# Unread matmuls at the head of TensorE's program, and another order of the first three weight slabs

## The reference, cut to what matters

```python
def hybrid_layer(x, ..., norm_g, w_in, ...):
    h = rms_norm(x, norm_g)          # x * rsqrt(mean(x*x) + 1e-6) * g
    z = h @ w_in                     # 1024 x 14848 columns, cut into eleven parts
    (c_glu, c_gate, r_q, r_k, r_v, ...) = split(z)
    y_conv = conv_module(c_glu, ...) # a * sigmoid(b), 31 taps, layer norm, silu
    y_ret = retention_branch(r_q, r_k, r_v, ...)
    ...
```

## Time and profile before

| | |
|---|---|
| Median of three runs | 2975.7 us |
| Profiled execution, its own time | 2974.69 us |
| Its span, first to last instruction | 2972.9 us |
| Around the span | 1.8 us |
| TensorE busy | 2943.8 us (99%) |
| VectorE busy | 1893.7 us (64%) |
| GpSimd busy | 1439.3 us (48%) |
| ScalarE busy | 1284.4 us (43%) |
| HBM traffic | 91 GB/s over the span |

### The profile page before, as it was taken

The page is one execution under the profiler, slowest core; times in us unless marked ns, Lnnn a source line. Parts: engine busy times, 40 slices in busy tenths (PEclk is TensorE's granted clock), DMA queues, the critical chain, the costliest instruction groups (busy, mean ns, idle before and its releaser), DMA issues.

```text
span 2972.9 us, 43739 instructions
## 1 busy us (share of the span) xinstructions
PE 2943.8 (99%) x15008; PEld 2456.0 (83%) x15008; DVE 1893.7 (64%) x2852; ACT 1284.4 (43%) x2068; POOL 1439.3 (48%) x1056
## 2 busy tenths in 40 slices
PE   8999999999999999999999999999999999999998
PEld 6888888878888888888887888888888888798997
DVE  7985577874524598577697634367772343784756
ACT  4233333484332423333347633246563323553634
POOL 5443443455555444443355555543444445555745
PEclk9999999999999999999999999999999999999999
DMA  4322322213333332222221233332223323333322
GB/s 153 99 72 77 92 78 83 88 44 100 92 99 102 120 99 80 90 84 71 81 90 58 78 97 102 92 121 71 78 71 99 106 79 120 99 100 100 108 92 86
DMA packets 73870, 271.34 MB, mean 91 GB/s; under 512 B 8192, under 2 KB 9088, under 8 KB 73088
## 3 DMA queue, kind: packets, MB, share of 16 engines
q1 hardware_dynamic: 70560, 254.84, 27.9%
q10 hardware_dynamic: 3168, 14.61, 1.4%
HBM read 264.17 MB, written 5.24 MB: 91 GB/s over the span
## 4 chain that ended last, share of the span: by engine, by line
PE 85%; issue 7%; POOL 5%; DVE 1%; ACT 1%; DVEq 0%; POOLq 0%; ACTq 0%
PE gem L574 15%; PE gem L576 15%; PE gem L575 15%; POOL wlo L471 5%; PE xp L1149 2%; PE xp L1150 2%; PE xp L1151 2%; PE gem L1009 2%; PE gem L1011 2%; PE gem L1010 2%; PE gem L701 2%; PE gem L699 2%; PE gem L700 2%; PE gem L819 2%; PE gem L821 1%
## 5 line engine op out<-in xcount | busy, mean ns | idle before, releaser
L471 POOL TENSOR_TENSOR wlo<-raw,whi 128x512 fp32r<-128x512 f32 x820 | 1135.4, 1407 | 1357.0 <-ACT whi L1234 1357.0
L1234 ACT ACTIVATE whi<-raw 128x1024 fp32r<-128x1024 f32 x410 | 432.6, 1057 | 493.9 <-PE gem L576 332.6
L574 PE MATMUL gem<-zhi,whi 128*128 128x512 f32 x1312 | 512.1, 390 | 0.3 <-DVE zlo L2006 0.3
L576 PE MATMUL gem<-zhi,wlo 128*128 128x512 f32 x1312 | 510.7, 389 | 0.0
L575 PE MATMUL gem<-zlo,whi 128*128 128x512 f32 x1312 | 510.5, 389 | 0.0
L574 PE MATMUL gem<-hhi,whi 128*128 128x512 f32 x1104 | 430.2, 390 | 0.0
L576 PE MATMUL gem<-hhi,wlo 128*128 128x512 f32 x1104 | 429.6, 389 | 0.0
L575 PE MATMUL gem<-hlo,whi 128*128 128x512 f32 x1104 | 429.5, 389 | 0.0
L574 PEld LDWEIGHTS gem<-zhi,whi 128*128 128x128 f32 x1312 | 246.3, 188 | 51.8 <-DVE zlo L2006 0.8
L576 PEld LDWEIGHTS gem<-zhi,wlo 128*128 128x128 f32 x1312 | 246.3, 188 | 51.6
L575 PEld LDWEIGHTS gem<-zlo,whi 128*128 128x128 f32 x1312 | 246.3, 188 | 50.8
(11 more groups left out here) (511 smaller groups left out, 6016.2 us busy)
## 6 DMA issues: line engine op xcount, KB each, us to landing
raw<-in_slabs SPq DMA_DIRECT2D x446, 512.0 KB, 3.6
U<-in_slabs SPq DMA_DIRECT2D x32, 512.0 KB, 3.7
U<-in_x SPq DMA_DIRECT2D x4, 512.0 KB, 6.6
U<-in_x ACTq DMA_DIRECT2D x1, 2048.0 KB, 10.1
xsave<-U ACTq DMA_DIRECT2D x1, 2048.0 KB, 6.7
U<-xsave ACTq DMA_DIRECT2D x1, 2048.0 KB, 10.0
out_y<-yr SPq DMA_DIRECT2D x8, 256.0 KB, 2.2
tab<-in_tab_ret ACTq DMA_DIRECT2D x2, 512.0 KB, 4.8
```

What stands on the lines that cost most here:

```text
L471: part = pool.tensor_tensor(wlo[:, k % 4, c], raw[:, k % 2, c], whi[:, k % 4, c].bitcast(f32), O.subtract)
L574: pe.matmul(o, wh, hi, start=(n == 0), stop=False)
L576: mm = pe.matmul(o, wl, hi, start=False, stop=(n == len(terms) - 1))
L1234: act.activation(whi[:, k % 4, :], raw[:, k % 2, :], A.Copy).then_inc(hi_done, 1)
```

## The change

TensorE executes 24 matmuls of the 128x128 constant of ones with itself (float32, 128 columns) into the first 128 columns of bank 3 of `xp`, as soon as that constant is set and ahead of its wait for the rounded copy; nobody reads the result. And the order of the first slabs becomes: rows 0 to 7 of slab 0, each as it arrives; rows 0 to 4 of slab 1; the square sum; rows 5 to 7 of slab 1; slab 2; slab 3. No other engine's list is changed.

```diff
+WARM = 24
...
             pe.sem_inc(slab_done, 1)
             pe.wait_ge(consts, 1)
+            for n in range(WARM):
+                pe.matmul(xp[:, 3, 0:P], ones[:, :], ones[:, :], start=True, stop=True)
             pe.wait_ge(ones_ready, 1)
...
                 else:
-                    plain_rows(0, 0, 5, arriving=True)
+                    plain_rows(0, 0, NT, arriving=True)
                     plain_rows(1, 0, 5)
                     square_sum(L, 0)
-                    plain_rows(0, 5, NT, arriving=True)
                     plain_rows(1, 5, NT)
                     plain_rows(2, 0, NT)
                 plain_rows(3, 0, NT)
```

## The result

The changed kernel took 2980.1 us in the median of 22 runs (2979.1 to 2980.8), the kernel before 2974.6 us in 22 runs (2974.3 to 2976.2). The ratio is 1.0017 with a 95% interval of 1.0011 to 1.0023: slower by 0.17% (the medians differ by 5.5 us), less than the 0.2% named in the prediction, and inside the stated range of 2976.9 to 2981.6. The forecast was +4.0 us. The span of the profiled execution grew from 2972.9 to 2978.2, by 5.3 us.

What follows compares the result with a forecast made beforehand. TensorE, busy 99%, was taken as the bound, with VectorE a second limit at bank 2. Matmuls 0, clock 0, TensorE's idle time +2.0, VectorE's lateness +2.0: 2975.7 + 4.0 = 2979.7 us, range 2976.9 to 2981.6.

Steps and rivals of the forecast that it cites:

- The 24 matmuls cost nothing, and end near 9: At TensorE's start, 48 records fit the 8.8 us wait for tile 0, ending between 6.5 and 12.8: cost 0.
- a rise in the middle: Within the 24 matmuls, the clock rises after some 4 us: 17 records take 4 us, the other 31 take 3.6.
- The estimate of 7.8 us at the upper level: For the 24 matmuls at the head: four float32 passes of about 81 ns each, against 5.6 us by the row.
- The clock gives nothing: Rows 0 to 2 of slab 0 shorten to 0.68 from 1.3 us, but TensorE then waits for tiles: gain 0.
- 0 for the clock: The clock's term in the forecast sum, for rows 0 to 2 at the start: no gain on the path.
- The rival of the clock that stays down: At the start, matmuls fail to raise the clock, still lower at 12.8: +6.2, 2981.9 us or more; chance 0.10.
- The order costs TensorE 2.0 us itself: Waiting for slab 0's rows 5 to 7 before slab 1 starts the fifth slab at 38.85 instead of 36.87.
- VectorE's lateness comes through at bank 2: At the value products, VectorE, 4.0 us late from the square sum, releases bank 2 late: +2.0 more for TensorE.
- one of about 2 us: Announced sign: a new wait of TensorE for VectorE at the value products, about 2 us, near 130.5.
- The matmuls do nothing at all: Rival: the clock falls back before tile 0, rows 0 to 2 unchanged, loss still 4.0; shares the forecast's 0.62.

Runs made afterwards that it cites:

- the filled kernel: The changed kernel plus 2, 2, 2, 6, 6 and 2 further unread matmuls behind rows 0 to 5 of slab 0; median 2978.6 us, ratio 1.0013.
- the one with only the chain late: Against the old order with 24 matmuls and gaps filled: square sum moved behind rows 5 to 7 of slabs 0 and 1; median 2978.6 us, ratio 1.0013.

## Why the prediction was right, and where it was off

**The number.** The total was nearer than the reasoning deserved. The forecast of 2979.7 us lies 0.4 under the measured 2980.1, but it stood on a median of 2975.7, 1.1 us above that of the 22 later runs; the change itself was forecast at +4.0 and measured at +5.5. That the two misses nearly cancel is luck.

**The 24 matmuls cost nothing, and end near 9.** Right: 8.81, for 8.8 us of idle start. The measured time for the whole train, 7.8 us, is within the bounds of 5.6 and 11.3, and the estimate of a rise in the middle was close.
The estimate of 7.8 us at the upper level that the prediction drew from the Trainium skill (page "TensorE: Matmul & The Clock Gate", section "Back-to-back issue gap") meets the same number by chance: the first 7 records took 1.66 us (0.98 to 2.64), 0.237 each, which is the lower level, and the other 41 took 0.15 each in the mean.

**The clock gives nothing.** Right as to the gain: with and without the matmuls the new order takes 2980.1 and 2980.3 us. But the sum says "0 for the clock", and lets a loss come only from a clock that is still down at 12.8. That is **the step that failed**: it priced the clock's rise and not its fall behind row 3. All rows after 13.35 were taken at the upper level, because in the trace of the kernel before they were; but there slab 1 filled the waiting time of tiles 5 to 7, and the change empties that stretch, while the short rows 0 to 2 leave more waiting ahead of it. Measured: the level fell at 15.9 and was back at about 22.7, the square sum came 1.6 us later than forecast, and the span is 1.4 us longer than with the gaps filled.

**The rival of the clock that stays down** had the right resource and the wrong moment. Its +6.2 lies nearer to the measured 5.3 of span and 5.5 of the medians than the forecast's 4.0 does, but its condition, the lower level still there at 12.8, was not met. The fall came behind rows whose single waits were 1.5 us or less, with TensorE busy 4.86 of 7.80 us.
The page "TensorE: Matmul & The Clock Gate" of the Trainium skill, section "Why this matters for your kernels", warns of idle gaps between bursts of matmuls, of gaps longer than any that stood here between the head's first matmul and the fall. The runs agree as to the direction, and they show that it isn't enough to look at the longest gap.

**The order costs TensorE 2.0 us itself.** Right: 38.81 and 38.88 for the fifth slab where the clock stays up, against 36.87; 40.43 where it falls.

**VectorE's lateness comes through at bank 2.** Right, as shown by the filled kernel (130.52 for 130.55) and by the one with only the chain late. In the form of the wait I was off: I announced one of about 2 us and missed that bank 0 is late as well (0.58 and 0.91 in the changed kernel, and 0.56 and 0.88 in the filled one, for a sum that the restarts complete to 2). That VectorE makes next to nothing up on its way is shown by the filled kernel: 4.05 us of lateness at the square sum (24.20 for 20.15) arrive as 3.9 at bank 2.

**The matmuls do nothing at all.** Not so: they did raise the clock for rows 0 to 2, which was worth nothing.

## What to carry to other kernels

When a loop waits for arriving pieces, price the clock for both directions: filling a wait with other work of the kernel, as the old order did with slab 1, also kept the clock up in the trace of the kernel before, and an order that takes this filling away loses twice. A fall can be diagnosed cheaply by filling the gaps with unread matmuls and looking whether the loss goes away. And an engine at 64% of the span can still be the next bound: look for the place where a buffer is released a tenth of a microsecond ahead of its use.

## What the runs showed of the hardware that was not expected

The clock came down within a stretch of separate short waits: busy 4.86 of 7.80 us ahead of the fall in the changed kernel, 2.33 of the last 3.70 us up to 16.3 in the one with the order alone; with 7.13 of 7.80 us it stayed up. The busy share alone does not decide: the kernel before kept the level in its trace with 5.46 of the same 7.80 us, while the one with the order alone, busy for 5.62 of them, lost it soon after, at 16.7. Once down it stayed so for 6.8 us in each of the two kernels, and for 3.4 us in the one with the matmuls alone, whose work was without gaps from 15.4 on. And the times of a whole program spread less where it doesn't happen: the five kernels whose clock stayed up in their traces have their 11 runs within 0.2 to 0.6 us of each other, those of the kernel before spread over 1.5 to 1.9 us, and those of the changed kernel over 1.7.
